# Four hand-overs between stages and the last expert unit rearranged in a two-block transformer kernel

## The reference, cut to what matters

```python
def first_block(x, ...):
    h = h + hybrid_mixer(rms_norm(h, norm1_w[layer]), ...)
    h = h + expert_choice_ffn(rms_norm(h, norm2_w[layer]), w_router[layer], ...)
    return rms_norm(h, final_norm_w)

def hybrid_mixer(n, ...):
    # gated delta rule in 8 heads, SSD in 16 heads, both directions
    gates, z = ...                                    # columns of n @ w_in
    y = (y_fw + y_bw + ssd_D * x_ssd) * jax.nn.silu(z)
    mixed = jnp.concatenate([o_gdn, rms_norm(y)], axis=-1)
    return jnp.einsum('blm,md->bld', mixed, w_out)

def expert_choice_ffn(n, w_router, w_gate, w_up, w_down):
    aff = jax.nn.softmax(n @ w_router, axis=-1)
    vals, idx = lax.top_k(jnp.swapaxes(aff, 1, 2), cap)   # 16 experts, 64 tokens each
    ...                                                   # gather, swiglu, add back

def moe_swiglu(h, router, wg, wu, wd):                    # 8 experts of width 1408
    vals, idx = lax.top_k(t @ router, TOP_K)              # 2 of 8 for each token
    gates = jax.nn.softmax(vals, axis=-1)
    for e in range(N_EXPERTS_2):
        out = out + combine[:, e:e + 1] * swiglu(t, wg[e], wu[e], wd[e])
# last lines of the second block:
        h = layer_norm(ALPHA * h + mix, ln1_g[i], ln1_b[i])
        f = moe_swiglu(h, router[j], ...)
        h = layer_norm(ALPHA * h + f, ln2_g[i], ln2_b[i])
```

## Time and profile before

| | us |
|---|---|
| median of 3 runs | 3258.61 (3257.73 to 3263.88) |
| profiled execution | 3259.85 |
| span of its profile | 3257.9 |
| TensorE matmuls busy | 2973.9 (91%) |
| TensorE weight loads busy | 1832.2 (56%) |
| VectorE busy | 1039.9 (32%) |
| ScalarE busy | 546.9 (17%) |
| GpSimd busy | 221.3 (7%) |

### The profile page before, as it was taken

One profiled execution on the slowest core, in us unless ns is written; L12 is line 12 of the kernel. 1 busy time (PEld: TensorE's weight loads), 2 busy tenths in 40 slices (PEclk: granted clock), 3 DMA queues, 4 the chain that ended last, 5 costly groups with the idle time before them and its releaser, 6 DMA issues. The chain is left out here.

```text
span 3257.9 us, 43583 instructions
## 1 busy us (share of the span) xinstructions
PE 2973.9 (91%) x18330; PEld 1832.2 (56%) x18330; DVE 1039.9 (32%) x1913; ACT 546.9 (17%) x1248; POOL 221.3 (7%) x204
## 2 busy tenths in 40 slices
PE   8998898998779979989999999999999599999895
PEld 4544787554333338867578884478775244444342
DVE  5666655653221234631300002119212211111013
ACT  3222322221111121133000000011340000000001
POOL 0001321340000000011000000000010000000000
PEclk9999899999879989999999999999999799999998
DMA  3411000116379921202012241012020615547926
GB/s 114 106 52 43 4 16 29 39 42 242 142 306 430 426 100 57 93 26 117 0 52 77 77 170 62 0 72 101 29 91 1 269 45 206 232 174 321 399 74 258
DMA packets 79954, 414.77 MB, mean 127 GB/s; under 512 B 10771, under 2 KB 16275, under 8 KB 64068
## 3 DMA queue, kind: packets, MB, share of 16 engines
q1 hardware_dynamic: 68028, 384.75, 29.9%
q10 hardware_dynamic: 8328, 15.40, 1.9%
q0 software_dynamic: 3456, 12.58, 1.0%
HBM read 383.69 MB, written 29.02 MB: 127 GB/s over the span
## 5 line engine op out<-in xcount | busy, mean ns | idle before, releaser
L3249 PE MATMUL pgu<-gu,xg 128*64 128x320 f32 (+1 forms) x2560 | 393.6, 463 | 8.0 <-POOLq L3192 5.6
L2884 PE MATMUL pp<-feat,lead 128*128 128x264 f32 x1408 | 315.9, 388 | 2.0 <-DVEq L2898 2.0
L3249 PEld LDWEIGHTS pgu<-gu,xg 128*64 128x64 f32 x2560 | 181.0, 137 | 205.8 <-issue 130.2
L2884 PEld LDWEIGHTS pp<-feat,lead 128*128 128x128 f32 x1408 | 269.1, 191 | 48.6 <-DVEq L2898 2.2
L372 PE MATMUL proj<-feat,w 128*128 128x512 f32 x576 | 255.9, 597 | 2.6 <-PEq L153 2.6
L2462 PE MATMUL ring<-feat,lead 128*128 128x264 f32 x1024 | 245.2, 401 | 3.0 <-PEq L2250 1.5
L2462 PEld LDWEIGHTS ring<-feat,lead 128*128 128x128 f32 x1024 | 201.0, 198 | 42.6 <-issue 6.8
L2462 PE MATMUL ring<-feat,w 128*128 128x264 f32 x896 | 208.3, 390 | 0.0
L3256 PE MATMUL py<-down,hm_t 128*64 128x512 f32 x880 | 200.1, 603 | 7.7 <-POOLq L3192 7.7
L2462 PEld LDWEIGHTS ring<-feat,w 128*128 128x128 f32 x896 | 169.9, 192 | 31.5 <-issue 3.1
L372 PEld LDWEIGHTS proj<-feat,w 128*128 128x128 f32 x576 | 107.4, 191 | 124.6 <-issue 124.6
(11 more groups left out here) (468 smaller groups left out, 3441.9 us busy)
## 6 DMA issues: line engine op xcount, KB each, us to landing
gu<-in_moe_gu SPq DMA_DIRECT2D x16, 3072.0 KB, 13.5
gu<-in_moe_gu SPq DMA_DIRECT2D x16, 2560.0 KB, 15.9
ring<-in_w_gate SPq DMA_DIRECT2D x16, 2048.0 KB, 13.7
ring<-in_w_up SPq DMA_DIRECT2D x16, 2048.0 KB, 15.3
ring<-in_w_down SPq DMA_DIRECT2D x16, 2048.0 KB, 17.6
w<-in_w_in SPq DMA_DIRECT2D x15, 2048.0 KB, 7.9
down<-in_moe_down SPq DMA_DIRECT2D x8, 3072.0 KB, 18.7
lead<-in_ffn_up SPq DMA_DIRECT2D x22, 1024.0 KB, 4.9
```

The costliest lines, as they stand in the source:

```text
L2884: last = pe.matmul(pp[:, b, a, half, 0:HALF], w[:, b, a, k * P:(k + 1) * P], core.feat[:, k, half * HALF:(half + 1) * HALF], start=k == 0, ...
L3249: last = pe.matmul(pgu[half(h), part, 0:n], xg[:, k, :], w[:, k, h, :], start=k == 0, stop=k == DK - 1)
```

## The change

It has five parts.

**A.** `Z_LATE` goes from 2 to 3. The pairs of units are shifted by one, so that the first period with units has one (unit 0), and the following ones have (1, 2), (3, 4) and so on. The third late unit goes into bank `pi` at the start of `ssd_and_output`.

```diff
-    Z_LATE = 2
+    Z_LATE = 3
...
-        z_from = GH + 2 - z_units // 2
+        z_from = GH + 2 - (z_units + 1) // 2
 
         def z_of(n):
-            return (2 * (n - z_from), 2 * (n - z_from) + 1) if n >= z_from else (None, None)
+            last = 2 * (n - z_from)
+            return last - 1 if last > 0 else None, last if last >= 0 else None
...
-                    for u, bank in zip(range(Z_UNITS - Z_LATE, Z_UNITS), (proj, pst)):
+                    for u, bank in zip(range(Z_UNITS - Z_LATE, Z_UNITS), (proj, pst, pi)):
                         gate_weights.make_z(pe, u, bank[:, 0:gate_weights.ZW])
...
-                        pe.wait_ge(gate_weights.z_out, Z_UNITS - 1)
+                        pe.wait_ge(gate_weights.z_out, Z_UNITS - Z_LATE + 1)
```

```diff
 # TensorE, in ssd_and_output
+                def turn_rows(t):
+                    pe.wait_ge(row_scaled, t + 1)
+                    if t >= 2:
+                        pe.wait_ge(row_moved, 2 * (t - 1))
+                    for k in range(DK):
+                        last = pe.transpose(row_out(t, k), core.o_acc[:, t, k * P:(k + 1) * P], ident)
+                    last.then_inc(row_turned, 1)
+
                 for t in range(TILES):
                     pe.wait_ge(out_read, t + 1)
                     contract(1, 0, t)
                     contract(1, 1, t).then_inc(out_made, 1)
+                    if t:
+                        turn_rows(t - 1)
+                turn_rows(TILES - 1)
 # ScalarE
+                def move_rows(t):
+                    act.wait_ge(row_turned, t + 1)
+                    for k in range(DK // 2):
+                        last = act.activation(core.feat[:, k, tl(t)], row_out(t, k), ACT.Copy, scale=row_gain(k))
+                    last.then_inc(row_moved, 1)
+
+                for t in range(TILES):
+                    act.wait_ge(out_read, TILES + t + 1)
+                    if t:
+                        act.wait_ge(row_squared, t)
+                    act.activation(row_scratch, core.hid[:, t, :], ACT.Square, accum_out=rstat[:, 0, t:t + 1]).then_inc(row_squared, 1)
+                    act.wait_ge(row_meaned, t + 1)
+                    act.activation(rstat[:, 2, t:t + 1], rstat[:, 1, t:t + 1], ACT.Sqrt).then_inc(row_root, 1)
+                    act.wait_ge(row_scaled, t + 1)
+                    act.dma_start(A["choice_rows"][tl(t), :], core.o_acc[:, t, :]).then_inc(route.stored, 16)
+                    if t:
+                        move_rows(t - 1)
+                move_rows(TILES - 1)
 # VectorE
                 for half in range(2):
                     for t in range(TILES):
...
                         dve.tensor_tensor(h, h, out[t][:, :], ALU.add).then_inc(out_read, 1)
+                        if half:
+                            scale_rows(t)
+                            if t:
+                                move_rows(t - 1)
+                move_rows(TILES - 1)
 # SP, in expert_choice_route
+            @block.sync
+            def _(sp):
+                sp.wait_ge(choice.stored, 16 * TILES)
+                weights.first_loads(sp)
```

```diff
     def first_loads(self, sp):
-        sp.dma_start(self.router[:, :, :], self.A["router_2"].rearrange("(k p) e -> p k e", p=P)).then_inc(self.route_in, 16)
-        sp.dma_start(self.row[:, :], self.A["index_row"].to_broadcast([P, P])).then_inc(self.route_in, 16)
         for part in range(2):
             self.load(sp, 0, part)
...
                 weights.first_loads(sp)
                 sp.wait_ge(weights.rows_in, 32)
-                for part in range(2, PARTS):
-                    weights.load(sp, 0, part)
```

```diff
 # route_top_two, VectorE
+                do(dve.tensor_scalar(wt[:, 2, 0:1], units_f[:, UNITS + 1 + NX:], float(UT), None, ALU.mult))
+                do(dve.tensor_scalar(placed[:, :, :], placed[:, :, :], wt[:, 2, 0:1], None, ALU.subtract))
+                for a in range(2):
+                    out = hit if a else weights.share
+                    do(dve.tensor_tensor(out[:, :, :], each(row[:, 0:UT], TILES), over(placed[:, :, a], UT), ALU.is_equal))
+                    do(dve.tensor_tensor(out[:, :, :], out[:, :, :], over(weight[:, :, a], UT), ALU.mult))
+                dve.tensor_tensor(weights.share[:, :, :], weights.share[:, :, :], hit[:, :, :], ALU.add).then_inc(weights.shared, 1)
 # expert_ffn, GpSimd
                 pool.wait_ge(all_stored, 1)
+                last = last_unit(pool)
+                for part in range(2):
+                    pool.wait_ge(part_done[part], last + 1)
+                    pool.sem_inc(got_free, 1)
+                pool.wait_ge(got_free, 2)
                 for t in range(TILES):
                     for a in range(2):
                         pool.indirect_dma_start(out=got[:, t, a, :], ...
 # ScalarE
-                with act.Fori(0, total) as s:
...
+                last = last_unit(act)
+                with act.Fori(0, last) as s:
+                    gates(s)
...
                     act.sem_inc(y_free, 1)
-                act.wait_ge(rows_in, total * 32 + 64)
                 act.sem_inc(all_stored, 1)
+                gates(last, more=False)
+                act.wait_ge(rows_in, last * 32 + 64)
 # TensorE
+                turn_rows(0)
+                last = last_unit(pe)
+                with pe.Fori(0, last) as s:
+                    unit(s)
+                unit(last, final=True)
+                pe.wait_ge(share_out, 1)
+                pe.wait_ge(y_out, last + 2)
+                for t in range(TILES):
+                    if t >= 2:
+                        pe.wait_ge(combined, 2 * TILES + t - 1)
+                    for h in range(2):
+                        added = pe.matmul(pgu[:, t % 2 * 2 + h, :], share_t[half(h), t * P:(t + 1) * P], y[half(h), :], start=True, stop=True)
+                    added.then_inc(last_added, 1)
 # VectorE
+                unit(last, final=True)
+                dve.wait_ge(enlarged, TILES + 1)
+                combine(0)
+                combine(1)
+                rows_out(last)
+                combine(2)
+                combine(3)
...
-                combine(0)
+                combine_last(0)
                 for t in range(1, TILES):
-                    combine(t)
+                    combine_last(t)
                     finish(t - 1)
                 finish(TILES - 1)
```

181 lines of the change are left out of this document (91 added, 90 removed).

## The result

| | before | after |
|---|---|---|
| median of the runs, us | 3259.48 (4 runs, 3257.73 to 3263.88) | 3236.98 (4 runs, 3236.25 to 3240.25) |
| span of the profile | 3257.9 | 3235.5 |
| TensorE matmuls busy | 2973.9 | 2981.4 |

The ratio is 0.993, with a 95% interval of 0.9917 to 0.9944: the change saves 22.5 us. The prediction said 33.7 us and 3225 us, with a range up to 3235. It named the right direction and missed the size: the measured time lies 2 us above its range. The same kernel on another chip gave 0.9916 (0.9902 to 0.9929), 27 us.

A forecast was written before the change was run, and what follows sets the result against it. TensorE was taken to bound the kernel, so gains lay in its waits and between stages. -13.9 - 4.6 - 4.3 - 1.9 - 9.0 = -33.7 us from 3258.6 gave 3225 us, range 3216 to 3235.

The forecast's parts named there:

- A: Gates of z in `gated_delta`: three waits and two slow units go, dropped unit gains, late unit costs; -13.9 us.
- So all three waits go: TensorE's waits for z's weights in `gated_delta` vanish, with two slow units: together 15.3 us.
- (1): Clock rival: a new 2.3 us idle and units staying partly slow leave A at -8; 3231 us; chance 0.13.
- (2): New DMA wait: first experts' gather lands in 10.8 us, scatter takes its whole 2.6; 3230 to 3231 us; chance 0.14.
- (5): One wait for z remains and gathers come behind the last unit: A -8, E 0; 3240 us; chance 0.03.
- (4): Slower: instructions arrive piece by piece at TensorE's loop exit, last unit at lower clock; 3265 us; chance 0.02.
- the dropped unit: Unit removed at the start of the first changed period in `gated_delta`: gain 1.3 us, new idle 2.3 us.
- B: Second norm of the first block: path from last add to router 8.6, 6.6 won, 2.0 lost; -4.6 us.
- The +2.0 for a late gather: First experts' first gather lands later, overlapping expert weight loads by about 2 us; between 0 and 6.5.
- C: Second router's tables loaded one block earlier: -6.0 us, less 1.7 (0 to 2.6) for a delayed scatter; -4.3 us.
- D: Four loads moved past a block's end behind the second scatter: TensorE starts sooner, assuming 2.4 us slack; -1.9 us.
- E: Last unit taken out of the loop: gathers no longer wait for it, first gather at 3211.5; -9.0 us.

The follow-up runs named there:

- part A alone: The kernel before with only part A of the change (three late units of z, pairs shifted): 3254.86 us, ratio 0.998 to the kernel before.
- TensorE kept at work: Changed kernel with 10 matmuls without a reader ahead of the last tile's turns and 8 behind: 3238.49 us, ratio 0.9924 to the kernel before.
- direct waits: Changed kernel, GpSimd's loop one unit shorter, TensorE waiting for the last expert's weights itself, VectorE adding three tiles ahead of y's copy: 3232.64 us.

## Why the prediction missed

**A is the step that failed**, by 7.8 us of the 11 that are missing. Its first half was right: the three waits and two slow units went, worth 15.3 as computed and 15.2 to 15.7 in the leads. What failed is that the sum has no term for the loads in their new place: "So all three waits go" was taken as their whole price, and the rest put at nothing. The prediction placed each load in the 20 us "of a period's other work" and asked only when the load would be there, not what that work needed of the same DMA engines. It needed its instructions. The two stalls beside the loads with what followed took back 2.7 and 2.6 us in the trace of part A alone; with the load in four paced transfers the changed kernel got 4.8 us back at the two places and kept 3.7. The last period, where the third stall stands without a load, took another 1.1 us of the lead in after (0.8 and 2.1 in the two kernels with the load in four), and no cause of that was tested. Why a block of instructions waits for the end of one load of 1 MB stays open too. None of the rivals had it: (1) charged the clock, (2) and (5) looked elsewhere, and (4), the one rival on instructions, placed them at the loop's exit, where nothing happened. The smaller errors of A: the dropped unit gave 0.3 us or nothing instead of 1.3, since VectorE's chain set the next steps too, and the low clock behind the three idles of 0.88 us, 1.6 us, which is the execution's and not the change's. The late unit cost 2.2 where 2.7 stood.

**B** came out at 4.3 beside 4.6 by luck: two errors cancel. The path to the router was right to 0.1 us (8.6). The +2.0 for a late gather was absent in the changed kernel, and 0.9 of it came when the router was fast. In its place stood 1.5 us in the router's products at the low clock, which the prediction did not look for although TensorE idles 2.5 and 1.55 us there, and 0.8 us more by the time the first experts are under way. That 0.8 is not shown to be B's: the trace of A alone, which has the old code there, loses 0.8 us against before in the same stretch.

The term for the late gather was therefore tested only in the kernel with TensorE kept at work: 0.9 us for an overlap of about 2, nearer to the 1 that was worked out from the Trainium skill's rule on round-robin queues (DMA: Bandwidth & Descriptors, Queues, rings and completion order) than to the 2 that was taken from the row. The working behind that 1 has a slip: 2.5 us is all that half a megabyte takes at half of 428 GB/s, and the increase over the full rate is 1.2.

**C and D**: the router's 6.0 us came (5.8), D's 1.9 came (2.0). The scatter's delay was 2.9 us, beyond the upper end of 2.6 that was set, and D had 1 us less of slack than the 2.4 it was given.

**E**: 7.6 beside 9.0. The steps are compared on the clock of the kernel before, by adding to the times of after the 14.82 us by which it led at the start of the last unit. The last weights then land at 3210.5, as assumed. GpSimd took 1.7 us from there to the first gather, not 0.8 (1.0 by the sum's own times), so that the gather stands at 3212.3 where 3211.5 was computed, and the first combine at 3219.0 beside 3218.3. The copy of y stands at 3225.0 beside 3223.5: VectorE waited 0.72 us more for the second tile's gathers, for which nothing was charged. These two, 0.7 each, are the missing 1.4. The store of the unit before the last, "long landed" in the prediction, landed about 7 us ahead of the last weights, and in the kernel with direct waits it was what the gathers waited for. The prediction also left out that the last unit has no table load, 2.3 us on TensorE, which the adds behind the gathers hide. Rival (4), the loop's exit, did not occur: there is no idle of TensorE between the loop and the last unit.

**The clock** in a single profile misled twice, both times in the kernel before: the slow unit behind the third wait is there in all three other traces with the old order of z, and the low stretch at the head of `ssd_and_output` in 8 of 14. Between the two profiles of the changed kernel the leads differ by up to 6 us on the way and by 3 at the end, so a term of 1 or 2 us read from one pair of profiles is not certain.

## What to carry to other kernels

A load that a wait is moved away from still runs somewhere: ask what else comes by DMA in those microseconds, the engine's own instructions among it, above all where it issues many small products. If a stall without a releaser follows, cut the transfer in four and look again before anything else is moved; here the stalls shrank in the traces, but the gain was too small for the timed median of that kernel alone. And where an engine idles a few microseconds ahead of the next stage's first product, read the granted clock there and put its price into the sum; but check what that product's successor waits for, since a faster stage can run into a transfer that the slow one had just let pass.

## What was not expected of the hardware

- One load of 1 MB (345 GB/s in the fullest of the windows shown) held back TensorE's next 16 KB of instructions until it had all but ended, and TensorE stood still for 1.6 to 1.9 us; beside four of 256 KB, queued together, it stood still for 0.5 to 0.9 us or not at all.
- TensorE also stood still for 1.37 us between small products with no load under way, until 1.5 us behind the end of a block of instructions.
- The low level of the clock (0.50) behind an idle of 3.2 to 3.6 us on TensorE came in three of four traces at the same place, and behind three idles of 0.88 us in a row in 8 of 14.
- Gathers of half a megabyte landed in 4.2 us at the least, 6.1 us (median) when eight follow each other, and 9.3 us when eight follow each other and the first of them run beside weight loads.
